# A router's product turned round and split over two halves of TensorE's columns, in a fused encoder layer

## The chip, the cores and the metric

The kernel runs on one core of one Trainium2 chip. All of it is one launch in float32. The metric is the device time of one execution in microseconds; the median over several runs is quoted, and a single execution that the hardware profiler recorded is used for the durations of parts.

## The reference

One layer of a hybrid encoder over 1024 tokens of width 1024: a state-space group and an attention group run side by side, their outputs are mixed by `W_o`, and the normalised sum goes through a mixture of 64 experts of which each token uses 6, plus one shared expert. The part around the change is this:

```python
mix = jnp.concatenate([s, a], axis=-1) @ w_o
x1 = _layer_norm(DEEPNORM_ALPHA * x + mix, ln1_g, ln1_b).astype(x.dtype)
# in _moe, xt = x1 as (1024, 1024):
scores = jax.nn.sigmoid((xt @ w_router).astype(jnp.float32))   # w_router: (1024, 64)
choice = scores + router_bias
# best 4 of 8 groups of experts, then the best 6 experts; weights from scores
...
shared = (jax.nn.silu(xt @ ws_gate) * (xt @ ws_up)) @ ws_down
out = _layer_norm(DEEPNORM_ALPHA * x1 + routed + shared, ln2_g, ln2_b)
```

## The kernel before, in words

The kernel has three stages divided by barriers: projection with attention and state-space scan, then mixing, first norm and routing (`mix_norm_route`), then the experts (`moe_experts`). Each engine has its own program; the order inside an engine is the order written, and engines meet through semaphores (`then_inc`, `wait_ge`). A wait holds back everything behind it on its engine.

In `mix_norm_route` the tokens go by in eight tiles of 128, `t` = 0 to 7. What belongs to a tile:

- `turn_o(t)` on TensorE and `keep_oT(t)` on ScalarE turn the attention output; `mix(t)` makes `p_m`, 16 matmuls of 512 columns: 8 with the turned attention output, then 8 with the state-space output. A float32 matmul is two records in the trace, so a mix is 32 records.
- `norm(t)` on VectorE makes `x1` for the tile. In it the variance goes to ScalarE, whose `deviation(t)` (L1363) takes the square root, and comes back.
- `turn_x(t)` on TensorE (L1274) transposes `x1` in eight blocks into `p_x`; ScalarE copies it to `k.x1T` (L1391).
- `route(t)` on TensorE (L1284) is the router's product: eight matmuls with the tile's `x1T` block as weights (128 by 128) and 64 columns of `w_r` moving, added up in `p_log`, tokens on the partitions. ScalarE's sigmoid (L1397) makes `score`.
- `route(t)` on VectorE picks groups and experts from `score`, makes `member` and the entries' weights; `rank(t)` on TensorE (L1291, L1293) counts tokens per expert; `place(t)` on VectorE (from L1463) turns the rank into a place, and GpSimd scatters the entries (L1225).
- `shared(n, part)` on TensorE (L1094, through `shared_gate_up`) is a quarter of the shared expert's hidden layer in two parts of 16 records each.

TensorE's loop over `t` is: `turn_x(t)`, `turn_o(t + 3)` while there is one, `mix(t + 2)`, `rank(t - 1)`, `route(t)`. In the last two steps there is no mix left, and the order is `turn_x(t)`, `shared(t - 6, 0)`, `rank(t - 1)`, `route(t)`, `shared(t - 6, 1)`. Then come `rank(7)`, one more counting product (L1342) that waits for VectorE's `place(7)` to have read `p_rank`, the other four parts of `shared`, and the transposes of the finished table.

ScalarE's loop is: copy of `x1T` for `t`, `keep_oT(t + 3)`, `deviation(t + 1)` while there is one, the sigmoid of `t`, and in the last two steps the sigmoid of the shared expert's gate. VectorE's is: `norm(t + 1)`, (`hidden(0)` in the last step,) `place(t - 1)`, `route(t)`. SyncE stores `x1` and, when all mixes are through, starts the loads of the first experts' weights into a ring of four places.

Of the kernel before, what the change touches and what calls it, by code (L numbers as in the profile page):

```python
# [6 lines left out]
f32 = mybir.dt.float32  # L7
i32 = mybir.dt.int32
u32 = mybir.dt.uint32
ALU = mybir.AluOpType  # L10
ACT = mybir.ActivationFunctionType
AX = mybir.AxisListType

P = 128
# [5 lines left out]
KD = D // P  # L20
# [11 lines left out]
N_EXPERTS = 64  # L32
# [1082 lines left out]
def mix_norm_route(nc, k):  # L1115

    with ExitStack() as ctx:
        sb, ps, sem = makers(nc, ctx, "mix", k.held)
        w_o = k.mix_w
        w_r = sb("w_r", [P, KD, N_EXPERTS], f32)  # L1120
# [40 lines left out]
        p_x = ps("p_x", [P, KD, P])  # L1161
        p_o = ps("p_o", [P, 512])
        p_log = ps("p_log", [P, 512])
        p_rank, p_log = p_o[:, 0:N_EXPERTS], p_log[:, 0:N_EXPERTS]

        wr_in, ln_in = sem("wr_in"), sem("ln_in")
        blank_done, blank_d, dest_done, scattered = sem("blank_done"), sem("blank_d"), sem("dest_done"), sem("scattered")
# [3 lines left out]
        x_back = [sem(f"x_back{t}") for t in range(T)]  # L1171
        o_turned, oT_done, mixed, mix_read = sem("o_turned"), sem("oT_done"), sem("mixed"), sem("mix_read")
        var_done, std_done, x1_done = sem("var_done"), sem("std_done"), sem("x1_done")
        x_turned, xT_act, logits = sem("x_turned"), sem("xT_act"), sem("logits")
        score_done, member_done, ranked, rank_read, own = sem("score_done"), sem("member_done"), sem("ranked"), sem("rank_read"), sem("own")
        gu_done, sig_done, h_done = sem("gu_done"), sem("sig_done"), sem("h_done")
# [61 lines left out]
        def _(pe):  # L1238
# [9 lines left out]
            def mix(t):  # L1248
                if t == 0:
                    pe.wait_ge(k.mix_w_in, 16)  # L1250
                if t >= 2:
                    pe.wait_ge(mix_read, 2 * t - 2)
                if t == 1:
                    pe.wait_ge(z_sig, 4)
                pe.wait_ge(oT_done, t + 1)
                for half in range(2):
                    cols = slice(half * 512, (half + 1) * 512)
                    for kk in range(4):
                        nc.tensor.matmul(p_m[:, t % 2, cols], oT[:, t % 2, kk, :], w_o[:, 4 + kk, cols], start=(kk == 0), stop=False)
                for half in range(2):  # L1260
                    cols = slice(half * 512, (half + 1) * 512)
                    for kk in range(4):
                        if t == 0 and half == 0:
                            pe.wait_ge(sT_done, kk + 1)
                        last = nc.tensor.matmul(p_m[:, t % 2, cols], k.sT[:, kk, t * P:(t + 1) * P], w_o[:, kk, cols],
                                                start=False, stop=(kk == 3))
                    last.then_inc(mixed, 1)
# [9 lines left out]
            def route(t):  # L1277
                pe.wait_ge(xT_act, t + 1)
                if t == 0:
                    pe.wait_ge(wr_in, 32)  # L1280
                else:
                    pe.wait_ge(score_done, t)
                for kk in range(KD):
                    last = nc.tensor.matmul(p_log, k.x1T[:, kk, t * P:(t + 1) * P], w_r[:, kk, :], start=(kk == 0), stop=(kk == KD - 1))  # L1284
                last.then_inc(logits, 1)

            def rank(t):
                pe.wait_ge(member_done, t + 1)
# [24 lines left out]
            mix(0)  # L1313
            turn_o(2)
            mix(1)
            def shared(n, part):
                if n == 0:
                    pe.wait_ge(k.ws_in, 48)
                if n >= 2:
                    pe.wait_ge(h_done, n - 1)  # L1320
                last = shared_gate_up(nc, k, n, part, p_m[:, n % 2, :])
                if part:
                    last.then_inc(gu_done, 1)

            for t in range(T):
                turn_x(t)
                if t + 3 < T:
                    turn_o(t + 3)
                if t + 2 < T:
                    mix(t + 2)  # L1330
                else:
                    pe.wait_ge(mix_read, 2 * t + 2)
                    shared(t + 2 - T, 0)
                if t:
                    rank(t - 1)
                route(t)
                if t + 2 >= T:
                    shared(t + 2 - T, 1)
            pe.wait_ge(rank_read, T - 1)
# [11 lines left out]
            for g in range(NQ):  # L1351
                last = nc.tensor.transpose(p_x[:, g, 0:COLS], spread[:, g, :, :].rearrange("b q i -> b (q i)"), k.ident[0:COLS, 0:COLS])
            last.then_inc(table_turned, 1)

        @block.scalar
        def _(act):
            def keep_oT(t):
                act.wait_ge(o_turned, t + 1)
                nc.scalar.activation(oT[:, t % 2, :, :].rearrange("p k t -> p (k t)"), p_o[:, :], ACT.Copy).then_inc(oT_done, 1)

            def deviation(t):
                act.wait_ge(var_done, t + 1)
                nc.scalar.activation(std[:, t % 2:t % 2 + 1], mv[:, t % 2, 1:2], ACT.Sqrt).then_inc(std_done, 1)  # L1363

            def gate(n):
                act.wait_ge(gu_done, n + 1)
                if n >= 2:
                    act.wait_ge(h_done, n - 1)
                nc.scalar.activation(sig[:, n % 2, :], p_m[:, n % 2, 0:512], ACT.Sigmoid).then_inc(sig_done, 1)

            def open_gate(m):
                act.wait_ge(z_done, m + 1)
                if m == 0:
                    act.wait_ge(s_done, 4)
                nc.scalar.activation(k.glu_a[m], p_z[m % 2], ACT.Sigmoid, bias=k.glu_b[:, m:m + 1]).then_inc(z_sig, 1)

            gelu_sigmoid(nc, k, 1).then_inc(s_sig, 1)
            gelu_sigmoid(nc, k, 2).then_inc(s_sig, 1)
            nc.scalar.activation(k.glu_a[3], k.glu_s[3], ACT.Square).then_inc(squared, 1)
            keep_oT(0)  # L1380
            act.wait_ge(cubed, 1)
            gelu_sigmoid(nc, k, 3).then_inc(s_sig, 1)
            open_gate(0)
            keep_oT(1)
            for m in range(1, 4):
                open_gate(m)
            keep_oT(2)
            deviation(0)
            for t in range(T):
                act.wait_ge(x_turned, 2 * t + 2)  # L1390
                nc.scalar.activation(k.x1T[:, :, t * P:(t + 1) * P], p_x[:, :, :], ACT.Copy).then_inc(xT_act, 1)  # L1391
                if t + 3 < T:
                    keep_oT(t + 3)
                if t + 1 < T:
                    deviation(t + 1)
                act.wait_ge(logits, t + 1)
                nc.scalar.activation(score[:, t % 2, :], p_log, ACT.Sigmoid).then_inc(score_done, 1)  # L1397
                if t + 2 >= T:
                    gate(t + 2 - T)
            gate(2)  # L1400
            gate(3)

        @block.vector
        def _(dve):
# [90 lines left out]
            for m in range(4):  # L1495
                dve.wait_ge(z_sig, m + 1)
                nc.vector.tensor_tensor(k.sT[:, m, :], k.glu_s[m], k.glu_a[m], ALU.mult).then_inc(sT_done, 1)
            dve.wait_ge(blank_done, 1)
            norm(0)
            for t in range(T):  # L1500
# [506 lines left out]
```

## Time and profile before

| | us |
|---|---|
| median of 3 runs (1530.87 to 1533.76) | 1531.8 |
| the profiled execution | 1530.07 |
| its span | 1528.2 |
| TensorE busy in the span | 1408.0 |
| VectorE busy | 793.8 |
| ScalarE busy | 367.7 |
| GpSimd busy | 612.5 |

The mixing and routing stage takes from about 500 to 732 us of the span, the expert stage all that is behind it. The granted TensorE clock was 0.98 of full speed on average. Times in the rows below are microseconds from the start of the span; a record of TensorE overlaps the next one, so what a group takes is read from its start to the start of the next group, not from its own duration.

### The profile page before, as it was taken

To read this page: it belongs to the slowest core of one execution; us is meant where nothing else is said; L and a number is where in the kernel's file an instruction comes from. 1 tells how busy PE (TensorE), PEld (TensorE's weight loads), DVE (VectorE), ACT (ScalarE), POOL (GpSimd) and SP (SyncE) were. 2 spreads that over 40 slices of the span, in tenths; PEclk is the share of its full clock that TensorE was granted. 3 is DMA by queue.
4 is the path that set the end of the run, shared out by engine and by line. 5 is a ranking of instruction groups with operands and counts; after the bars stand their busy time and mean duration, and the time that the engine had idled before them with its cause. 6 is when DMAs were issued, how large, how long until landed. Compare 5 with 4: busy or idle time off the path is not lost.

```text
span 1528.2 us, 17423 instructions
## 1 busy us (share of the span) xinstructions
PE 1408.0 (92%) x5334; PEld 729.6 (48%) x5334; DVE 793.8 (52%) x1420; ACT 367.7 (24%) x737; POOL 612.5 (40%) x590
## 2 busy tenths in 40 slices
PE   6997999999998999999899999999999999999980
PEld 3544666666666445554344444444444444444430
DVE  3575788888887337884433333333242332323325
ACT  0213555555555312310000101001010100101015
POOL 0008445554430001343345545555554555545520
PEclk9999999999999999999999999999999999999995
DMA  9406101001103630033779999999999999999946
GB/s 233 64 36 75 18 11 19 15 16 19 41 17 123 248 138 29 29 118 135 265 263 370 371 367 370 355 373 361 376 359 371 356 356 374 360 371 362 325 105 234
DMA packets 115342, 321.98 MB, mean 211 GB/s; under 512 B 44390, under 2 KB 65534, under 8 KB 90338
## 3 DMA queue, kind: packets, MB, share of 16 engines
q1 hardware_dynamic: 91890, 261.99, 46.9%
q0 software_dynamic: 23408, 59.45, 16.0%
q8 instruction: 22, 0.36, 0.1%
q14 instruction: 22, 0.18, 0.0%
HBM read 276.45 MB, written 51.72 MB: 215 GB/s over the span
## 4 chain that ended last, share of the span: by engine, by line
DMA 40%; PE 5%; issue 4%; DVE 2%; POOLq 1%; ACT 0%; POOL 0%; ACTq 0%; SPq 0%
DMA sum_d<-moe_y,moe_idx 40%; PE moe_p_gu L1699 2%; PE moe_p_s L1735 2%; PE moe_p_y L1719 1%; DVE all_x_sb L1913 1%; DVE all_x_sb L1908 1%; DMA moe_xg<-x_d,moe_idx 1%; DMA all_x_sb<-sum_d 0%; POOLq L1641 0%; POOL moe_xg L1645 0%; POOL sum_d L1656 0%; POOLq L1682 0%; ACT moe_junk L1815 0%; DVE moe_y L1847 0%; POOLq L1642 0%
## 5 line engine op out<-in xcount | busy, mean ns | idle before, releaser
L1830 DVE STREAM_TRANSPOSE moe_xgT<-moe_xg 128x1024 f32<-128x1024 f32 x65 | 132.0, 2031 | 420.1 <-DMA moe_xg<-x_d,moe_idx 420.1
L1645 POOL DMA_INDIRECT moe_xg<-x_d,moe_idx x260 | 263.7, 1014 | 115.9 <-issue 60.4
L1719 PE MATMUL moe_p_y<-mixers_ring_b,moe_hT 128*128 128x512 f32 x520 | 233.9, 593 | 0.9 <-DVE moe_hT L1841 0.9
L1699 PE MATMUL moe_p_gu<-mixers_ring_b,moe_xgT 128*128 128x512 f32 x512 | 225.0, 593 | 0.0
L1656 POOL DMA_INDIRECT sum_d<-moe_y,moe_idx x65 | 105.7, 1626 | 244.3 <-DMA sum_d<-moe_y,moe_idx 207.5
L1767 ACT ACTIVATE moe_sig<-moe_p_gu 128x256 f32<-128x256 f32 x65 | 24.9, 383 | 585.6 <-PE moe_p_gu L1699 585.6
L1719 PEld LDWEIGHTS moe_p_y<-mixers_ring_b,moe_hT 128*128 128x128 f32 x520 | 98.8, 190 | 124.9 <-issue 123.8
L1699 PEld LDWEIGHTS moe_p_gu<-mixers_ring_b,moe_xgT 128*128 128x128 f32 x512 | 95.2, 191 | 107.1 <-issue 107.1
L1225 POOL DMA_INDIRECT slot_d<-all_entry,all_dest_i x48 | 48.3, 1007 | 224.9 <-DVE all_dest_i L1471 212.7
L709 PE MATMUL att_p_s<-latents_kT,att_qT 128*128 128x512 f32 x256 | 122.8, 603 | 1.1 <-ACT att_v L879 0.7
L1699 PE MATMUL moe_p_gu<-mixers_ring_a,moe_xgT 128*128 128x512 f32 x272 | 119.5, 592 | 0.0
L1699 PE MATMUL moe_p_gu<-mixers_o,moe_xgT 128*128 128x512 f32 x256 | 113.9, 598 | 0.9
L969 DVE TENSOR_REDUCE att_nmax<-att_p_s 128x1 f32<-128x1024 f32 x64 | 78.3, 1224 | 36.0 <-PE att_p_s L709 32.6
L223 POOL TENSOR_TENSOR all_x_sb<-all_x_sb 128x512 f32<-128x512 f32 x32 | 33.8, 1056 | 120.4 <-ACT all_x_sb L209 118.0
L922 ACT ACTIVATE att_prT<-att_p_t 128x512 f32<-128x512 f32 x128 | 69.4, 595 | 40.8 <-PE att_p_t L831 40.8
L1699 PEld LDWEIGHTS moe_p_gu<-mixers_ring_a,moe_xgT 128*128 128x128 f32 x272 | 50.6, 191 | 57.4 <-issue 57.4
L1699 PEld LDWEIGHTS moe_p_gu<-mixers_o,moe_xgT 128*128 128x128 f32 x256 | 47.4, 190 | 57.0 <-issue 57.0
L831 PEld LDWEIGHTS att_p_t<-all_const,att_pr 128*128 128x128 f32 x512 | 59.1, 141 | 29.2 <-issue 29.2
L883 ACT ACTIVATE att_pr<-att_p_s,att_nmax 128x1024 f32<-128x1024 f32 x64 | 70.9, 1108 | 2.3 <-DVE att_nmax L969 2.1
L841 PE MATMUL att_p_o<-att_prT,att_v 128*64 128x128 f32 x1024 | 64.2, 279 | 6.6 <-ACT att_prT L922 6.5
L1773 ACT ACTIVATE moe_y<-moe_p_y,shared_block_w 128x512 f32<-128x512 f32 x65 | 44.7, 688 | 100.7 <-PE moe_p_y L1719 99.4
L831 PE MATMUL att_p_t<-all_const,att_pr 128*128 128x128 f32 x512 | 66.4, 273 | 1.8 <-ACT att_prT L922 1.8
(324 smaller groups left out, 1931.6 us busy)
## 6 DMA issues: line engine op xcount, KB each, us to landing
mixers_ring_b<-in_we_down_dram SPq DMA_DIRECT2D x65, 1024.0 KB, 9.3
mixers_ring_b<-in_we_gate_dram SPq DMA_DIRECT2D x32, 1024.0 KB, 10.2
mixers_ring_b<-in_we_up_dram SPq DMA_DIRECT2D x32, 1024.0 KB, 16.4
mixers_ring_a<-in_we_gate_dram SPq DMA_DIRECT2D x17, 1024.0 KB, 10.0
mixers_ring_a<-in_we_up_dram SPq DMA_DIRECT2D x17, 1024.0 KB, 15.2
mixers_o<-in_we_gate_dram SPq DMA_DIRECT2D x16, 1024.0 KB, 10.1
mixers_o<-in_we_up_dram SPq DMA_DIRECT2D x16, 1024.0 KB, 16.5
moe_xg<-x_d,moe_idx POOLq DMA_INDIRECT x260, 6.9
```

The costliest lines, as they stand in the source:

```text
L709: last = nc.tensor.matmul(p_s[:, t % 2, half * 512:(half + 1) * 512], qT[:, u, t * P:(t + 1) * P], kT[:, u, half * 512:(half + 1) * 512], ...
L831: last = nc.tensor.transpose(p_t[:, j, :], pr[:, t % 2, j * P:(j + 1) * P], k.ident)
L841: last = nc.tensor.matmul(p_o[s * DV:(s + 1) * DV, 0:P], v[:, u, j, :], prT[:, s, j, :], start=(j == 0), stop=(j == T - 1))
L883: nc.scalar.activation(pr[:, t % 2, :], p_s[:, t % 2, :], ACT.Exp, bias=nmax[:, t % 2:t % 2 + 1], accum_out=total[:, t:t + 1]).then_inc(pr ...
L922: nc.scalar.activation(prT[:, t % 2, 4 * half:4 * half + 4, :], p_t[:, 4 * half:4 * half + 4, :], ACT.Copy).then_inc(pT_kept, 1)
L969: nc.vector.tensor_reduce(nmax[:, t % 2:t % 2 + 1], p_s[:, t % 2, :], AX.X, ALU.max, negate=True).then_inc(topped, 1)
L1225: nc.gpsimd.indirect_dma_start(k.slot_d[:, :], bass.IndirectOffsetOnAxis(ap=k.dest[:, n:n + 1], axis=0), k.entry[:, t, q, :], None).then_i ...
L1645: nc.gpsimd.indirect_dma_start(xg[:, u, g, :], None, x1_quarters, bass.IndirectOffsetOnAxis(ap=idx[:, c, g:g + 1], axis=0), bounds_check=N ...
L1656: nc.gpsimd.indirect_dma_start(k.sum_d[:, :], bass.IndirectOffsetOnAxis(ap=idx[:, c, NQ:NQ + 1], axis=0), y[:, u, :], None, compute_op=ALU ...
L1699: last = nc.tensor.matmul(p_gu[:, u, :], xgT[:, u, kk, :], k.moe_gu[v][:, :, kk * F:(kk + 1) * F], start=(kk == 0), stop=(kk == KD - 1))
L1719: last = nc.tensor.matmul(p_y[:, half * 512:(half + 1) * 512], hT[:, u, kk, :], k.moe_dn[v][:, kk * D + half * 512:kk * D + (half + 1) * 512],
L1830: nc.vector.transpose(xgT[:, u].rearrange("p k (g i) -> p g k i", g=NQ), xg[:, u].rearrange("p g (j k) -> p g k j", k=KD)).then_inc(x_turn ...
```

## The change

The router's product is turned: `w_r` (128 by 64) becomes the weights and the tile's `x1T` block (128 columns) moves. The eight blocks of the contraction go in turn to the lower and the upper half of the array's columns, so `p_lt` holds two half sums, each with experts on the partitions. ScalarE copies `p_lt` to `lt`, and a new product `add_halves(t)` with `lt` as weights and two identities of 64 stacked on each other (`both`) gives the sum, turned back, in `p_log`. VectorE builds `both` once. In steps 0 to 5 TensorE's `route(t)` moves to the middle of `mix(t + 2)`, and `add_halves(t)` takes its old place; in steps 6 and 7 `route(t)` stands ahead of `rank(t - 1)` and `add_halves(t)` behind it. ScalarE's copy stands behind `deviation(t + 1)` and ahead of the sigmoid.

```diff
-        p_rank, p_log = p_o[:, 0:N_EXPERTS], p_log[:, 0:N_EXPERTS]
+        both = sb("both", [P, N_EXPERTS], f32)
+        lt = sb("lt", [P, 2, P], f32)
+        p_rank, p_lt, p_log = p_o[:, 0:N_EXPERTS], p_log[:, P:2 * P], p_log[:, 0:N_EXPERTS]
...
                 pe.wait_ge(oT_done, t + 1)
+                routed = t - 2
                 for half in range(2):
                     cols = slice(half * 512, (half + 1) * 512)
                     for kk in range(4):
                         nc.tensor.matmul(p_m[:, t % 2, cols], oT[:, t % 2, kk, :], w_o[:, 4 + kk, cols], start=(kk == 0), stop=False)
+                if routed >= 0:
+                    route(routed)
                 for half in range(2):
...
                 for kk in range(KD):
-                    last = nc.tensor.matmul(p_log, k.x1T[:, kk, t * P:(t + 1) * P], w_r[:, kk, :], start=(kk == 0), stop=(kk == KD - 1))
-                last.then_inc(logits, 1)
+                    s = kk % 2
+                    last = nc.tensor.matmul(p_lt[s * N_EXPERTS:(s + 1) * N_EXPERTS, :], w_r[:, kk, :], k.x1T[:, kk, t * P:(t + 1) * P],
+                                            start=(kk < 2), stop=(kk >= KD - 2))
+                last.then_inc(lt_done, 1)
+
+            def add_halves(t):
+                if t == 0:
+                    pe.wait_ge(both_done, 1)
+                pe.wait_ge(lt_kept, t + 1)
+                nc.tensor.matmul(p_log, lt[:, t % 2, :], both[:, :], start=True, stop=True).then_inc(logits, 1)
...
                     shared(t + 2 - T, 0)
+                    route(t)
                 if t:
                     rank(t - 1)
-                route(t)
+                add_halves(t)
                 if t + 2 >= T:
                     shared(t + 2 - T, 1)
...
                 if t + 1 < T:
                     deviation(t + 1)
+                act.wait_ge(lt_done, t + 1)
+                nc.scalar.activation(lt[:, t % 2, :], p_lt, ACT.Copy).then_inc(lt_kept, 1)
                 act.wait_ge(logits, t + 1)
                 nc.scalar.activation(score[:, t % 2, :], p_log, ACT.Sigmoid).then_inc(score_done, 1)
...
                 nc.vector.tensor_tensor(k.sT[:, m, :], k.glu_s[m], k.glu_a[m], ALU.mult).then_inc(sT_done, 1)
+            nc.vector.tensor_tensor(both[:, :], k.ident[:, 0:N_EXPERTS], k.ident[:, N_EXPERTS:], ALU.add).then_inc(both_done, 1)
             dve.wait_ge(blank_done, 1)
             norm(0)
```

## Rows read from the trace of the kernel before

**Rows 1.** Chain of waits from 500 us on: start, us, what

```profile
731.93 29.54 PE moe_p_s L1735 x64
...
782.23 10.96 DMA sum_d<-moe_y,moe_idx
```

**Rows 2.** One stretch, busy us (records) of PE, PEld, DVE, ACT, POOL; PEclk, DMA, GB/s

```profile
628.00:645.00 17.00, 17.00 (x64) 9.35 (x63) 14.19 (x49) 4.50 (x6) 6.09 (x6) 1.00 0.09 31
```

**Rows 3.** TensorE in order of time, steps 5 to 7: start, us, what, idle before

```profile
660.47 0.39 PE L1293 MATMUL mix_p_o<-mix_seen,all_const 128*128 128x64 f32 x2
660.70 1.95 PE L1284 MATMUL mix_p_log<-mix_w_r,mixers_ring_b 128*128 128x64 f32 x16
662.48 1.09 PE L1274 MATMUL mix_p_x<-all_const,all_x_sb 128*128 128x128 f32 x8
663.41 7.03 PE L1094 MATMUL mix_p_m<-mixers_ring_b,mix_gu 128*128 128x512 f32 x16
670.28 0.33 PE L1291 MATMUL mix_p_o<-mix_member,all_const 128*128 128x64 f32 x2
...
670.67 1.95 PE L1284 MATMUL mix_p_log<-mix_w_r,mixers_ring_b 128*128 128x64 f32 x16
672.46 7.09 PE L1094 MATMUL mix_p_m<-mixers_ring_b,mix_gu 128*128 128x512 f32 x16
...
687.13 0.33 PE L1291 MATMUL mix_p_o<-mix_member,all_const 128*128 128x64 f32 x2
...
698.00 0.44 PE L1342 MATMUL mix_p_o<-mix_seen,all_const 128*128 128x64 f32 x2 [1.21 <-DVE mix_hots L1463]
698.27 27.69 PE L1094 MATMUL mix_p_m<-mixers_ring_b,mix_gu 128*128 128x512 f32 x64
```

**Rows 4.** VectorE in order of time, the ranks of tiles 4 and 6

```profile
660.90 0.55 DVE L1463 TENSOR_TENSOR mix_hots<-mix_hot,mix_p_o 128x384 f32<-128x384 f32 x1 [1.24 <-PE mix_p_o L1293]
...
687.73 0.56 DVE L1463 TENSOR_TENSOR mix_hots<-mix_hot,mix_p_o 128x384 f32<-128x384 f32 x1 [0.27 <-PE mix_p_o L1293]
```

**Rows 5.** TensorE in order of time, attention, around L841

```profile
416.06 1.06 PE L745 MATMUL att_p_p<-mixers_ring_a,att_vsT 128*128 128x128 f32 x8
416.96 1.88 PE L709 MATMUL att_p_s<-latents_kT,att_qT 128*128 128x512 f32 x4
...
419.55 1.06 PE L745 MATMUL att_p_p<-mixers_ring_a,att_vsT 128*128 128x128 f32 x8
420.54 1.97 PE L841 MATMUL att_p_o<-att_prT,att_v 128*64 128x128 f32 x32
422.43 1.99 PE L709 MATMUL att_p_s<-latents_kT,att_qT 128*128 128x512 f32 x4
```

**Rows 6.** ScalarE in order of time; last, all copies of L908 (ns)

```profile
656.98 0.20 ACT L1363 ACTIVATE mix_std<-mix_mv 128x1 f32<-128x1 f32 x1 [7.88 <-DVE mix_rstd L1421]
...
673.81 0.20 ACT L1363 ACTIVATE mix_std<-mix_mv 128x1 f32<-128x1 f32 x1 [7.88 <-DVE mix_rstd L1421]
674.03 1.28 ACT L1397 ACT_TABLE_LOAD   x1
...
L908 ACT ACTIVATE att_oh<-att_p_o x32: 277/277/278, 155.5 to 496.1; 128x128 f32<-128x128 f32 x32
```

**Rows 7.** TensorE after waits; then stretches of 1 us, columns as in rows 2

```profile
139.25 0.63 PE L732 MATMUL att_p_p<-all_const,att_vs 128*128 128x128 f32 x4 [2.71 <-DVE att_vs L621]
...
149.95 2.04 PE L745 MATMUL att_p_p<-mixers_ring_a,att_vsT 128*128 x8 [4.00 <-DMA mixers_ring_a<-u_d]
...
500.17 1.08 PE L1245 MATMUL mix_p_o<-all_const,mixers_o 128*128 128x128 f32 x4 [3.37 <-PEq L1948]
...
155.00:156.00 1.00, 1.00 (x8) 0.59 (x5) 0.23 (x1) 0.51 (x2) 1.00 (x1) 0.94 0.00 0
506.00:507.00 1.00, 1.00 (x3) 0.41 (x2) 0.96 (x4) 0.00 (x0) 0.00 (x0) 0.65 1.03 426
735.00:736.00 1.00, 1.00 (x3) 0.32 (x2) 0.36 (x1) 0.00 (x0) 0.93 (x1) 0.80 1.00 418
```

More of the change, by code:

```diff
@@ L1173, in mix_norm_route @@
         var_done, std_done, x1_done = sem("var_done"), sem("std_done"), sem("x1_done")
+        both_done, lt_done, lt_kept = sem("both_done"), sem("lt_done"), sem("lt_kept")
         x_turned, xT_act, logits = sem("x_turned"), sem("xT_act"), sem("logits")
```

## Prediction

> **What bounds the kernel now.** I read the chain of waits first. From the barrier that closes the mixing and routing stage (called the stage below) it runs without a gap: 29.5 us of TensorE, then expert after expert a scatter whose landing sets the pace [rows 1]. Nothing behind the barrier is touched, and each load of expert weights there waits for a place that an earlier expert frees, so a stage that ends later or earlier moves the end by as much.
>
> Inside the stage I read the busy times by stretch: over a whole token tile TensorE works 17.00 of 17.00 us while VectorE works 14.19 and ScalarE 4.50 [rows 2]. So up to tile 5 only TensorE time counts. In steps 6 and 7 that is no longer true: instead of a mix of 32 wide records, the rank and the router's product have only 16 of them in front (663.41 to 670.28), and 16 behind (672.46) [rows 3]. VectorE has the same work as ever: from the rank of tile 4 (660.90) it runs without a gap, past the variance of tile 7 which ScalarE awaits until 673.81, to the rank of tile 6 at 687.73, for which it waits only 0.27 us [rows 4, 6]. Then TensorE itself waits 1.21 us for VectorE before its last gapless run of 27.69 us [rows 3]. What is late for that run is late at the barrier.
>
> **Part by part: the product itself.** Removed: 16 matmul records per tile, 660.70 to 662.48 = 1.78 us [rows 3], eight times. They stand one behind another, about 0.11 us each.
> Added, first: 16 records with 64-column weights, two for the lower half of the columns, two for the upper, and so on, each moving 128 columns. The trace of before holds this very pattern: the attention's weighted sum (L841) alternates the two halves in pairs of records with the same shapes, and its 32 records last from 420.54 to 422.43 [rows 5]. With (1.97 - 0.28) / 31 = 0.055 us per record (0.28 being about what one record lasts by itself: the 1.06 us of the eight records of L745 less seven steps of 0.11) the halves do run beside each other. 32 records are then 1.75 us, and 0.14 us is left for going back to whole-width matmuls. Going in costs too: L745 lasts 0.99 us ahead of L841 and 0.90 ahead of L709; and the first whole-width group behind it is 0.11 longer (1.99 against 1.88) [rows 5]. So my price c for one turned product is 16 x 0.055 + 0.14 + 0.09 + 0.11 = 1.22 us. Its floor is 0.87 (no cost of change of width); its ceiling is 16 records in a row at 0.11 plus 0.34, or 2.1 us. I take 1.22, since every term has its row.
> The Trainium skill (TensorEngine Tiling, Key Properties) says that a change of tiling mode drains TensorE, and under Theoretical Speedup that two tiles bring up to 2x; by the 2x alone c would be 1.78 / 2 = 0.89 and the sum at the end 3.1 us in place of 5.4. The rows show 0.34 us of cost at the changes of width, so the trace agrees with the drain and the 2x is not reached.
> Added, second: the product with the stacked identities, two records of 64 columns on whole-width weights, as the second matmul of a rank: 660.47 to 660.70 = 0.23 us [rows 3].
> Balance per tile where nothing waits: 1.78 - 1.22 - 0.23 = 0.33 us gained.
>
> **What hides the rest.** The one VectorE addition that builds the identities lies in the long wait for the first mix, over 2 us, and costs nothing. The copy of the half sums on ScalarE is 0.28 us by the same shape in the attention [rows 6]; in tiles 0 to 5 the turned product sits in the middle of a 13.7 us mix, so the copy has some 7 us until it is needed. It stands behind the next tile's deviation on ScalarE, which comes ahead of the rank there (656.98 to 657.18 in step 5, the rank ending at 660.70) [rows 3, 6]. Queues of DMAs: nothing is moved past SP's or POOL's issues.
>
> **The two steps where it isn't hidden.** Clock times are those of before; R is 660.70, where the rank of tile 4 is done. VectorE's run from there to the variance of tile 7 has no gap, so it stays tied to R [rows 4].
> Step 6 after the change: identities' product of tile 5 0.23, eight transposes 0.93 (662.48 to 663.41), first shared half 6.87 (663.41 to 670.28), turned product 1.22, rank 0.39 (670.28 to 670.67) [rows 3]: 660.70 + 9.64 = 670.34. Now comes the new wait. The sum of tile 6 needs ScalarE's copy, and in ScalarE's order that copy stands behind the deviation of tile 7, which waits for VectorE until 673.81 and takes 0.20 [rows 6]. 673.81 + 0.20 + 0.28 + some 0.05 of handing over = 674.34. TensorE stands still for about 3.8 us, since its last matmul drains until about 670.5; queued behind it is the second shared half. The product then takes 0.27 as a lone one (698.00 to 698.27), so that half starts at 674.61, where it started at 672.46: 2.15 us late. Before, the sigmoid stood behind the same deviation, but no TensorE instruction waited for it.
> The table of the sigmoid is loaded behind the deviation (674.03, 1.28 us) [rows 6]. I take it that it will stand behind the copy too, ahead of the sigmoid that it is for; ahead of the copy it would add 1.3 us, which I keep for the range.
>
> **The clock.** After a wait of 2.71 us four matmuls of 128 columns take 0.63 us in all, after one of 3.37 us they take 1.08: the granted clock is then 0.5, 1.2 GHz, the lower of its two levels. From the clock in stretches of 1 us it is back at 1.00 (2.4 GHz) at 506.7 and, after a wait of 4.00 us, at 155.1, that is 6.5 and 5.2 us after the restarts at 500.17 and 149.95; behind the barrier (731.93) it took until 735.4, 3.5 us [rows 1, 7]. A wait of 3.8 us lies between two that did it. Half of 5.1 us, their mean, is lost: 2.5 us (1.75 to 3.25).
> The Trainium skill (TensorE: Matmul & The Clock Gate, "Why this matters for your kernels") advises against idle gaps between bursts of matmuls, since the clock falls in them. The restarts of rows 7 agree; were it not so, the sum would be that of the first rival.
>
> Step 7: the half is over 2.15 + 2.5 = 4.65 us late. The turned product of tile 7 stands ahead of the rank of tile 6, where the old product stood behind it: another 1.22. The rank starts 5.87 us after 687.13 [rows 3]. VectorE, which waited 0.27 us for it, starts as much late [rows 4], and its work on the last tile leads to the one product (698.00) that TensorE waits for; TensorE's own work in between (0.39 + a copy's wait + 0.27 + 6.9 us) is shorter than the 10.87 us from 687.13 to 698.00, so VectorE's lateness is what counts. Against this stands what was gained up to R: 5 x 1.78 = 8.90 removed, 6 x 1.22 + 5 x 0.23 = 8.47 added (six turned products lie before R, five sums), so 0.43.
> Sum: 5.87 - 0.43 = 5.4 us longer. Against the profiled execution, 1530.07 us with a span of 1528.2 and 1.9 around it, that is 1535.5. The median of the runs is 1.7 above that execution, so I state 1531.8 + 5.4 = 1537.2, 0.35% slower. About 0.2%, 3.1 us, is what a measurement can tell from no change.
>
> **Rivals.**
> 1. The wait comes, the clock holds: 5.4 - 2.5 = 2.9 us, 1534.7. For it: one drop came only after 3.37 us, so the bound is near 3.8. Against: three of three such waits. Chance 0.16. It lies on the edge of 0.2%.
> 2. The halves take turns instead of running beside each other, so the change doesn't do what it says: c = 2.1. Before R 6 x 2.1 + 1.15 - 8.90 = 4.9 us lost, then 4.65 + 2.1 = 6.8: 11.6 us, 1543.4. Against it stands L841 with the same shapes. Chance 0.05.
> 3. Not slower: the new wait does not bite. It decides at 670.34: the copy would have to be through by then, 4.0 us ahead of where the deviation puts it, as if ScalarE did not keep its order or the last norm came sooner. TensorE would reach the rank of tile 6 0.66 us before 687.13, VectorE is ready only 0.27 sooner; total 0.3 + 0.4 gained with c = 1.22, 0.3 + 2.5 with c = 0.87: 1531.1 down to 1529.0. Against: the row of the deviation and the gapless VectorE. Chance 0.10, most of it within 0.2%.
> 4. The expert stage takes up or adds some us when it starts at another phase of its transfers: anywhere from 1530 to 1541. Chance 0.07; nothing in the chain speaks for it.
> The forecast has 0.62.
>
> **How the numbers follow.** The sum as a function of c is 7c - 3.1 (2.15 + 2.5 + c late, 8.90 - 6c - 1.15 gained). With c at 0.87 the forecast is 2.4 us less, with the clock at its dearest 0.75 more, with the table ahead 1.3 more. The forecast's own range is 1534.4 to 1539; with the first rival, the size of c and a spread of the runs of 1 to 2 us the range is 1533.3 to 1539.6. Slower by over 0.2%: 0.62, half of rival 1, rival 2, part of 4: 0.76. Same: 0.17. Faster: 0.07.
>
> **What would show it.** Right: the turned product in tiles 0 to 5 lasts about 1.0 us from its start to that of the mix's next matmul and the period of a tile falls by 0.3; an idle TensorE of about 3.8 us ahead of the identities' product of tile 6, released by ScalarE, and half the clock behind it; rank of tile 6 near 692.6; barrier 5 us later. Wrong: 16 records that take 1.7 us (rival 2), full clock in the second shared half of step 6 (rival 1), or that half starting before 672 (rival 3).

## The result and the profile after

The changed kernel takes 1537.1 us (median of 14 runs, 1534.98 to 1542.08) against 1531.8 us for the kernel before in the same rounds (14 runs, 1528.06 to 1533.76). The ratio is 1.0037, 95% interval 1.0027 to 1.0047: 0.37% slower. The profiled execution of the changed kernel took 1537.33 us with a span of 1535.4 us, 7.3 us more than that of before. The difference of the medians is 5.3. In the experiments one execution of e2_fill_wait took 3826 us and is left out of its numbers.

| us | before | after |
|---|---|---|
| the profiled execution | 1530.07 | 1537.33 |
| its span | 1528.2 | 1535.4 |
| TensorE busy | 1408.0 | 1411.1 |
| VectorE busy | 793.8 | 795.0 |
| ScalarE busy | 367.7 | 370.0 |
| from the first tile's transposes to the barrier | 172.0 | 179.0 |
| from the barrier to the end of the span | 796.3 | 796.2 |

The last two lines tell where to look: all of it is lost ahead of the barrier. The chain of waits of after takes the same steps behind it as in [rows 1] (start, us, what):

```profile
739.19 30.40 PE moe_p_s L1753 x64
...
790.35 11.48 DMA sum_d<-moe_y,moe_idx
```

A whole token tile, TensorE in order of time (start, us, what, idle before), around the turned product of tile 3:

```profile
610.24 1.09 PE L1280 MATMUL mix_p_x<-all_const,all_x_sb 128*128 128x128 f32 x8
...
611.60 7.03 PE L1263 MATMUL mix_p_m<-mixers_ring_b,mix_oT 128*128 128x512 f32 x16
618.57 1.09 PE L1291 MATMUL mix_p_log<-mixers_ring_b,mix_w_r 128*64 128x128 f32 x16
619.59 7.13 PE L1271 MATMUL mix_p_m<-mixers_ring_b,mixers_ring_a 128*128 128x512 f32 x16
626.56 0.33 PE L1305 MATMUL mix_p_o<-mix_member,all_const 128*128 128x64 f32 x2
...
626.95 0.39 PE L1299 MATMUL mix_p_log<-mix_both,mix_lt 128*128 128x64 f32 x2
627.18 1.09 PE L1280 MATMUL mix_p_x<-all_const,all_x_sb 128*128 128x128 f32 x8
```

The turned product takes 1.02 us to the next group's start (618.57 to 619.59), and each of the two mix groups around it 6.97 (611.60 to 618.57, 619.59 to 626.56), 0.10 us more than the 6.87 of a group without it [rows 3]. From the transposes of one tile to those of the next are 16.94 us (610.24 to 627.18); before, the same two transposes stand 17.28 us apart (611.08 to 628.36).

Steps 6 and 7 and what follows them, the same view; then, in a second fence, ScalarE and VectorE in order of time:

```profile
660.61 1.09 PE L1280 MATMUL mix_p_x<-all_const,all_x_sb 128*128 128x128 f32 x8
...
669.80 0.39 PE L1307 MATMUL mix_p_o<-mix_seen,all_const 128*128 128x64 f32 x2
673.95 0.69 PE L1299 MATMUL mix_p_log<-mix_both,mix_lt 128*128 128x64 f32 x2 [3.76 <-ACT mix_lt L1412]
674.43 9.62 PE L1094 MATMUL mix_p_m<-mixers_ring_b,mix_gu 128*128 128x512 f32 x16
683.89 1.06 PE L1280 MATMUL mix_p_x<-all_const,all_x_sb 128*128 128x128 f32 x8
...
692.77 0.43 PE L1305 MATMUL mix_p_o<-mix_member,all_const 128*128 128x64 f32 x2
...
701.04 0.41 PE L1305 MATMUL mix_p_o<-mix_member,all_const 128*128 128x64 f32 x2 [0.47 <-issue]
...
703.74 0.69 PE L1357 MATMUL mix_p_o<-mix_seen,all_const 128*128 128x64 f32 x2 [2.07 <-issue]
704.23 28.98 PE L1094 MATMUL mix_p_m<-mixers_ring_b,mix_gu 128*128 128x512 f32 x64
```

```profile
673.53 0.20 ACT L1378 ACTIVATE mix_std<-mix_mv 128x1 f32<-128x1 f32 x1 [9.46 <-DVE mix_rstd L1438]
673.64 0.26 ACT L1412 ACTIVATE mix_lt<-mix_p_log 128x128 f32<-128x128 f32 x1
673.91 1.28 ACT L1414 ACT_TABLE_LOAD   x1
...
693.47 0.56 DVE L1480 TENSOR_TENSOR mix_hots<-mix_hot,mix_p_o 128x384 f32<-128x384 f32 x1 [6.27 <-PE mix_p_o L1307]
```

TensorE stands still for 3.76 us in front of the halves' sum of tile 6 (L1299), until ScalarE's copy, which follows the deviation (673.53) without a gap. VectorE, which waited 0.27 us for the rank of tile 6 in [rows 4], now waits 6.27. Stretches of 1 us, columns as in [rows 2], show the half clock around both waits; by the same view it lasts from 672.7 to 679.5 and from 703.4 to 706.8 us:

```profile
673.00:674.00 1.00, 0.05 (x1) 0.05 (x1) 0.93 (x4) 0.45 (x3) 0.00 (x0) 0.50 0.00 0
...
680.00:681.00 1.00, 1.00 (x4) 0.49 (x3) 0.86 (x5) 0.00 (x0) 0.79 (x1) 1.00 0.95 360
703.00:704.00 1.00, 0.26 (x1) 0.26 (x2) 0.93 (x3) 0.00 (x0) 0.52 (x1) 0.71 0.00 0
...
705.00:706.00 1.00, 1.00 (x2) 0.34 (x1) 0.93 (x4) 0.00 (x0) 0.43 (x1) 0.50 0.00 0
```

### The profile page after: what moved, and what is told of

It is laid out like the page before. It is cut to its first block, busy times and chain, and to the rows that moved or that the text cites. A ratio compares the mean times of both kernels' runs of the same rounds, so it can differ in the third digit from the quotient of the medians.

```text
span 1535.4 us, 17465 instructions
## 1 busy us (share of the span) xinstructions
PE 1411.1 (92%) x5350; PEld 726.1 (47%) x5350; DVE 795.0 (52%) x1421; ACT 370.0 (24%) x745; POOL 613.5 (40%) x590
## 4 chain that ended last, share of the span: by engine, by line
DMA 39%; PE 6%; issue 3%; DVE 2%; POOLq 1%; ACT 0%; POOL 0%; ACTq 0%; SPq 0%
DMA sum_d<-moe_y,moe_idx 39%; PE moe_p_gu L1717 3%; PE moe_p_s L1753 2%; PE moe_p_y L1737 1%; DVE all_x_sb L1931 1%; DVE all_x_sb L1926 1%; DMA moe_xg<-x_d,moe_idx 1%; DMA all_x_sb<-sum_d 0%; POOLq L1659 0%; POOL moe_xg L1663 0%; PE moe_p_h L1725 0%; POOL sum_d L1674 0%; POOLq L1700 0%; ACT moe_junk L1833 0%; DVE moe_y L1865 0%
## 5 line engine op out<-in xcount | busy, mean ns | idle before, releaser
L841 PE MATMUL att_p_o<-att_prT,att_v 128*64 128x128 f32 x1024 | 65.4, 283 | 6.6 <-ACT att_prT L922 6.4
```

Source lines behind the costliest of these rows:

```text
L841: last = nc.tensor.matmul(p_o[s * DV:(s + 1) * DV, 0:P], v[:, u, j, :], prT[:, s, j, :], start=(j == 0), stop=(j == T - 1))
```

## The experiments

All kernels below were timed in rounds with the kernel before on the same chip. "To the barrier" is the time from the first tile's transposes to the barrier in the profiled execution; it leaves out what an execution spends elsewhere. Behind the barrier the profiled executions of the nine kernels below take from 793.4 to 798.0 us, though nothing there was changed, so a single span can't show an effect of 1 or 2 us, and the stretch to the barrier can. It is known from one execution of each kernel. The experiments were timed in four batches, each with its own median of the kernel before (1531.6 to 1532.4 us), so medians of different rows are compared by the ratio.

| run | tiles 0 to 5 | transposes of tile 6 to the barrier | to the barrier | median | ratio (95%) |
|---|---|---|---|---|---|
| before | 102.52 | 69.45 | 171.97 | 1531.8 | |
| after | 100.46 | 78.58 | 179.04 | 1537.1 | 1.0037 (1.0027 to 1.0047) |
| e2_fill_wait | 100.47 | 74.30 | 174.77 | 1536.7 | 1.0027 (1.0015 to 1.0039) |
| e3_one_half | 107.46 | 76.75 | 184.21 | 1544.4 | 1.0086 (1.0071 to 1.0100) |
| e1_copy_first | 100.47 | 74.12 | 174.59 | 1535.0 | 1.0022 (1.0012 to 1.0031) |
| e8_scatters_later | 100.46 | 75.06 | 175.52 | 1535.5 | 1.0024 (1.0015 to 1.0033) |
| e6_sum_later | 100.46 | 70.83 | 171.29 | 1532.7 | 1.0002 (0.9992 to 1.0013) |
| e4_before_tail | 102.52 | 68.01 | 170.53 | 1531.8 | 1.0000 (0.9991 to 1.0009) |
| e10_tail_only | 100.47 | 74.41 | 174.88 | 1533.6 | 1.0009 (0.9999 to 1.0018) |
| e7_sum_later_tail | 100.48 | 68.43 | 168.91 | 1529.1 | 0.9981 (0.9968 to 0.9993) |
| e9_split_part | 100.46 | 67.34 | 167.80 | 1527.6 | 0.9976 (0.9964 to 0.9987) |

**Is it the clock? (e2_fill_wait)** Four matmuls into `p_x`, whose contents nobody reads by then, fill TensorE's wait in step 6; the order is untouched.

```diff
                     rank(t - 1)
+                if t == T - 2:
+                    for i in range(4):
+                        nc.tensor.matmul(p_x[...], k.ws_gu[:, i, 0:P], k.x1T[:, i, 0:512], start=True, stop=True)
                 add_halves(t)
```

> The changed kernel with four float32 matmuls of 512 columns (8 records, 3.4 us) into the unused transposes' banks put into TensorE's wait of step 6; their result is overwritten unread. Theory (the wait costs 2.15 us by itself and 2.5 to 3 us by the half clock): the second shared half takes 6.9 us in place of 9.46, the total is 2.6 us less than the changed kernel, about 2.7 above the kernel before, 1534.5. Rival (the clock falls anyway, or its cost is made up for while VectorE works on): same time as the changed kernel, 1537.

TensorE in order of time:

```profile
669.18 3.65 PE L1353 MATMUL mix_p_x<-mixers_ring_b,mix_gu 128*128 128x512 f32 x8
673.10 0.43 PE L1299 MATMUL mix_p_log<-mix_both,mix_lt 128*128 128x64 f32 x2 [0.27 <-ACT mix_lt L1416]
673.37 7.08 PE L1094 MATMUL mix_p_m<-mixers_ring_b,mix_gu 128*128 128x512 f32 x16
680.29 1.05 PE L1280 MATMUL mix_p_x<-all_const,all_x_sb 128*128 128x128 f32 x8
...
700.13 0.43 PE L1361 MATMUL mix_p_o<-mix_seen,all_const 128*128 128x64 f32 x2 [2.07 <-issue]
700.40 27.68 PE L1094 MATMUL mix_p_m<-mixers_ring_b,mix_gu 128*128 128x512 f32 x64
```

The sum starts no earlier than the copy allows (673.10), and the group behind it takes 6.92 us (673.37 to 680.29) where it took 9.46 (674.43 to 683.89). So the 2.54 us are the clock's. To the barrier it is 2.8 us more than before; 2.7 was expected. The total does not follow: 1534.5 was expected, and the median of 1536.7 is the rival's 1537. The nine runs fall into 1531.1 to 1534.6 (four, the profiled one among them) and 1536.7 to 1538.8 (five). The profiled execution lacks the second stretch at half clock, although TensorE waits 0.46 and 2.07 us ahead of the 64 records as it does in the changed kernel (0.47 and 2.07): they take 27.68 us here and 28.98 there. Whether that stretch makes the upper group isn't shown.

**Do the halves run beside each other? (e3_one_half)** All eight blocks go to the lower half, the sum contracts over 64.

```diff
-                    s = kk % 2
+                    s = 0
...
-                                            start=(kk < 2), stop=(kk >= KD - 2))
+                                            start=(kk == 0), stop=(kk == KD - 1))
...
-                nc.tensor.matmul(p_log, lt[:, t % 2, :], both[:, :], start=True, stop=True).then_inc(logits, 1)
+                nc.tensor.matmul(p_log, lt[0:N_EXPERTS, t % 2, :], both[0:N_EXPERTS, :], start=True, stop=True).then_inc(logits, 1)
...
-                nc.scalar.activation(lt[:, t % 2, :], p_lt, ACT.Copy).then_inc(lt_kept, 1)
+                nc.scalar.activation(lt[0:N_EXPERTS, t % 2, :], p_lt[0:N_EXPERTS, :], ACT.Copy).then_inc(lt_kept, 1)
```

> The changed kernel with all eight blocks of the contraction on the lower half of the columns, and the sum taken over those 64 rows: turned as before, but nothing beside anything. Theory (the halves run beside each other, which is what makes 16 records cost 0.055 us each): the turned product costs 2.1 us a tile instead of 1.22, the period of a tile grows by 0.88, total by 7c - 3.1 = 11.6 us above the kernel before, or 9 if the shorter wait (2.9 us) no longer lowers the clock: 1541 to 1543.5. Rival (it is the 64-column weights that are cheap, not the two halves): time of the changed kernel, 1537.

```profile
657.65 1.96 PE L1291 MATMUL mix_p_log<-mixers_ring_b,mix_w_r 128*64 128x128 f32 x16
659.54 7.13 PE L1271 MATMUL mix_p_m<-mixers_ring_b,mixers_ring_a 128*128 128x512 f32 x16
...
680.44 0.43 PE L1299 MATMUL mix_p_log<-mix_both,mix_lt 64*128 64x64 f32 x2 [2.58 <-ACT mix_lt L1412]
680.80 7.13 PE L1094 MATMUL mix_p_m<-mixers_ring_b,mix_gu 128*128 128x512 f32 x16
687.77 1.05 PE L1280 MATMUL mix_p_x<-all_const,all_x_sb 128*128 128x128 f32 x8
```

The 16 records take 1.89 us where the two halves took 1.02. The same 16 records with the same shapes differ by 0.87 us only in where they go, so the halves run beside each other. The price of one turned product is then 1.89 + 0.20 for its two neighbours = 2.09, the prediction's ceiling of 2.1. The run is still dearer than expected: tiles 0 to 5 take 7.0 us more than in the changed kernel, 1.17 a tile where 0.88 was expected, and the median is 1544.4 us where 1541 to 1543.5 was. The other 0.3 us a tile lie around the sum, which now has only 64 rows: it takes 0.36 us to the next group (667.00 to 667.36) instead of 0.22, it starts 0.10 later behind the rank, and the transposes behind it last 0.06 longer. So this kernel pays for a second change of shape, and its total is not the price of the unsplit product alone.

**Take the copy out from behind the deviation (e1_copy_first).** ScalarE makes the copy first and the next tile's deviation after it.

```diff
-                if t + 1 < T:
-                    deviation(t + 1)
                 act.wait_ge(lt_done, t + 1)
                 nc.scalar.activation(lt[:, t % 2, :], p_lt, ACT.Copy).then_inc(lt_kept, 1)
+                if t + 1 < T:
+                    deviation(t + 1)
```

> The changed kernel with one edit: ScalarE's copy of the half sums stands ahead of the next tile's deviation instead of behind it. Theory (the wait of TensorE for that copy in step 6, and the half clock behind it, are the loss; with them gone VectorE, which had only 0.27 us to spare, sets the last steps): the wait of 3.76 us and the long shared half of 9.46 us go, the rank of tile 6 comes about 0.3 + 0.3 us ahead of the kernel before, total 0.6 us shorter than before, about 1531.2. Rival (the turned product ahead of the rank of tile 6, or the split of the mix, is the loss): the time stays 3 us or more above the kernel before.

GpSimd, ScalarE and TensorE in order of time:

```profile
670.61 0.97 POOL L1228 DMA_INDIRECT slot_d<-all_entry,all_dest_i  x1 [0.30 <-issue]
...
672.64 0.28 ACT L1410 ACTIVATE mix_lt<-mix_p_log 128x128 f32<-128x128 f32 x1 [8.93 <-remote]
...
672.97 0.43 PE L1299 MATMUL mix_p_log<-mix_both,mix_lt 128*128 128x64 f32 x2 [1.84 <-ACT mix_lt L1410]
673.25 8.78 PE L1094 MATMUL mix_p_m<-mixers_ring_b,mix_gu 128*128 128x512 f32 x16
681.86 1.06 PE L1280 MATMUL mix_p_x<-all_const,all_x_sb 128*128 128x128 f32 x8
```

A miss: 1531.2 us was expected and 1535.0 came, the rival's number but not for the rival's reason. The turned product was over by 670.54, ScalarE had nothing in front, and yet the copy began at 672.64, put down to no engine ("remote"). It begins 1.06 us after the end of GpSimd's last scatter, one of tile 4 (670.61 + 0.97 = 671.58). The copies of tiles 2 to 6 all came so, 1.6 to 2.3 us late and 0.96 to 1.10 us behind the last scatter; those of tiles 0, 1 and 7, with no scatter in flight, began at once. And the wait of only 1.84 us that was left still brought half clock: the group behind it took 8.61 us (673.25 to 681.86).

**Is it the scatters? (e8_scatters_later)** As e1_copy_first, and GpSimd's scatters of tiles 0 to 4 wait for the copy of the tile two later.

```diff
+                if t <= 4:
+                    pool.wait_ge(lt_kept, t + 3)
```

> The kernel with the copy ahead of the deviation, and GpSimd's scatters of tiles 0 to 4 held back until ScalarE's copy two tiles later is through, so that no scatter is under way at a copy. In the run without this the copies of tiles 2 to 6 began 1.6 to 2.3 us after the turned product was done and 1.0 us after GpSimd's last scatter; those of tiles 0, 1 and 7, with no scatter about, at once. Theory (a copy waits for the scatters, by whatever way): all copies begin within 0.1 us of the product, TensorE's wait in step 6 falls from 1.84 us to under 0.3, full clock behind it, total 0.6 us below the kernel before, 1531.2. Rival (the delay belongs to the copy's place in ScalarE's queue or to its bank of sums): the delays stay at 1.6 us or more, total 3.3 us above the kernel before.

```profile
670.16 0.28 ACT L1412 ACTIVATE mix_lt<-mix_p_log 128x128 f32<-128x128 f32 x1 [5.92 <-PE mix_p_log L1293]
...
670.53 0.39 PE L1301 MATMUL mix_p_log<-mix_both,mix_lt 128*128 128x64 f32 x2
670.76 7.09 PE L1094 MATMUL mix_p_m<-mixers_ring_b,mix_gu 128*128 128x512 f32 x16
677.68 1.05 PE L1282 MATMUL mix_p_x<-all_const,all_x_sb 128*128 128x128 f32 x8
...
688.53 0.28 ACT L1412 ACTIVATE mix_lt<-mix_p_log 128x128 f32<-128x128 f32 x1 [8.74 <-remote]
...
688.86 0.43 PE L1301 MATMUL mix_p_log<-mix_both,mix_lt 128*128 128x64 f32 x2 [1.65 <-ACT mix_lt L1412]
...
701.06 1.17 PE L1094 MATMUL mix_p_m<-mixers_ring_b,mix_gu 128*128 128x512 f32 x1
```

(ScalarE and TensorE in order of time.) On the delay the theory holds: the copies of tiles 0 to 6 now begin at once (670.16), TensorE has no wait at 670.53, the next group takes 6.92 us (670.76 to 677.68). On the time it doesn't: the scatters held back then run back to back until 686.25, the copy of tile 7 is late instead (688.53), TensorE waits 1.65 us there, and later 1.65 and 2.07 us more, with half clock behind. The median is 1535.5 us where 1531.2 was expected. So the delay was moved from tiles 2 to 6 to tile 7. That the start of this copy hangs on scatters in flight is shown by the two runs; how it does so is not.

**Let the sum come later instead (e6_sum_later).** The copy stays where the change put it; in step 6 TensorE draws the second shared half ahead of the sum.

```diff
+                if t == T - 2:
+                    shared(t + 2 - T, 1)
                 add_halves(t)
-                if t + 2 >= T:
+                if t + 2 > T:
                     shared(t + 2 - T, 1)
```

> The changed kernel with one edit: in step 6 TensorE does the second shared half ahead of the product that adds the halves, so that ScalarE's copy has 6.9 us more; ScalarE's order is the changed kernel's. Theory (the loss is TensorE's wait for the copy and the half clock behind it; without them VectorE, with 0.27 us to spare, sets the last steps): no wait and full clock in step 6, the rank of tile 6 is reached ahead of VectorE, total 0.6 us shorter than the kernel before, about 1531.2. Rival (some 3 us of the loss are elsewhere, in the last ranks or the expert stage, as the run with the copy ahead of the deviation could suggest): 3 us above the kernel before, 1535.

```profile
677.72 0.33 PE L1299 MATMUL mix_p_log<-mix_both,mix_lt 128*128 128x64 f32 x2
...
688.28 0.43 PE L1299 MATMUL mix_p_log<-mix_both,mix_lt 128*128 128x64 f32 x2 [0.81 <-ACT mix_lt L1414]
...
698.29 0.43 PE L1359 MATMUL mix_p_o<-mix_seen,all_const 128*128 128x64 f32 x2 [2.07 <-issue]
698.56 1.94 PE L1094 MATMUL mix_p_m<-mixers_ring_b,mix_gu 128*128 128x512 f32 x4
```

The wait of step 6 and its stretch at half clock are gone (677.72), and the 64 records at the end run at full clock although 2.07 us of waiting stand ahead of them here too. That is 7.75 us to the barrier less than after and 0.68 less than before (0.6 expected). In the total this kernel can't be told from the kernel before (1532.7 against 1532.4 in the same rounds, where 0.6 less was expected). The order of two calls carries the whole net loss: of the 9.13 us that the changed kernel loses from the transposes of tile 6 to the barrier, 1.38 are left, and the 2.06 gained in tiles 0 to 5 cover them.

**The last steps (e4_before_tail, e10_tail_only).** In the kernel before and in the changed one, the first half of a later shared part (8 records) goes ahead of `rank(7)` and the second half behind it, ahead of the last counting product, so that neither waits for VectorE.

```diff
+            pe.wait_ge(h_done, 1)
+            gate_part(2, 0, 4)
             rank(T - 1)
+            gate_part(2, 4, KD)
...
-            for n in range(2, 4):
-                for part in range(2):
-                    shared(n, part)
+            shared(2, 1)
+            for part in range(2):
+                shared(3, part)
```

> The kernel before with TensorE's last steps put in another order: the first part of the shared expert's third quarter is drawn ahead, half of it in front of the rank of tile 7 and half behind, in front of the last counting product. Theory (TensorE's 1.21 us of waiting for VectorE there is on the path, and VectorE and the scatters have room): that wait goes, total 1.2 us less, about 1530.6. Rival (the later table, scatters and VectorE become the bound, or the expert stage takes it up): same or above 1531.8.

> The changed kernel (copy behind the deviation, halves' sum ahead of the second shared half) with one edit: TensorE's last steps in the order of the run that reordered them in the kernel before, so that neither the rank of tile 7 nor the last counting product waits for VectorE. In the changed kernel these two waited 0.47 and 2.07 us, and 64 records behind them took 1.3 us more than in the kernel before, the product ahead of them 0.2 more, at half the clock. Theory (the 1.5 us of the second stretch at half clock hangs on these two waits, and most executions of the changed kernel have it): 2.6 us of waits and 1.5 us of clock go, from the first tile's transposes to the barrier 179.0 - 4.1 = 174.9 us; total 1537.1 - 4.1 = 1533.0. Rival 1 (the second stretch is in few executions, and the changed kernel's median has little of it): the profiled execution as above, but a total of 1534.0 to 1534.7. Rival 2 (the second stretch comes from the first, 20 us earlier, and not from the waits): no waits, but still half clock behind 703 us, 176.4 us to the barrier, 1534.5.

In the kernel before it takes 1.44 us off the way to the barrier (1.2 expected) and nothing that the total can show: 1530.6 was expected, 1531.8 came. In the changed kernel it takes 4.16 us off (174.88; 174.9 expected) and 3.6 us off the median; by the ratios, each against the kernel before in its own rounds, it is 0.28% or 4.3 us. From the rank of tile 6 to the barrier it is 41.95 us against 46.42, 4.47 less: 2.54 of waits, 1.5 of clock, 0.4 more than I can assign; the slow group of step 6 took 0.33 more in this execution:

```profile
674.90 0.69 PE L1299 MATMUL mix_p_log<-mix_both,mix_lt 128*128 128x64 f32 x2 [3.75 <-ACT mix_lt L1421]
675.38 9.95 PE L1094 MATMUL mix_p_m<-mixers_ring_b,mix_gu 128*128 128x512 f32 x16
...
705.12 0.33 PE L1305 MATMUL mix_p_o<-mix_member,all_const 128*128 128x64 f32 x2
...
709.00 0.33 PE L1366 MATMUL mix_p_o<-mix_seen,all_const 128*128 128x64 f32 x2
```

Step 6 still has its wait of 3.75 us and a slow group, but behind it nothing waits, and from 701 to 716 us the clock is 1.00. Rival 2 of that run (the second stretch comes from the first) is out by three more traces: e1_copy_first has the first stretch without the second (27.68 us for the 64 records), and e3_one_half and e8_scatters_later have the second (29.38 and 29.15 us) without the first. How many executions of the changed kernel have the second stretch is not shown: the ratio's interval, 0.9999 to 1.0018, is 3 us wide and holds both the theory (1533.0) and most of rival 1 (1534.0 to 1534.7).

**Both, and the rest of step 7 (e7_sum_later_tail, e9_split_part).** The first is e6_sum_later with the last steps in the new order. The second also draws half of the second shared half of step 7 (4 of 8 matmuls) ahead of the sum of tile 7.

```diff
+                if t == T - 1:
+                    up_part(1, 0, 4)
                 add_halves(t)
                 if t + 2 > T:
-                    shared(t + 2 - T, 1)
+                    up_part(1, 4, KD).then_inc(gu_done, 1)
```

> The same, and TensorE's last steps in the other order that was tried on the kernel before (half of a shared part ahead of the rank of tile 7, half behind it). Theory (VectorE held back what the turned product saves; here TensorE has work for that time): from the rank of tile 4 to the barrier 67.6 us where the kernel before took 71.2, and 0.3 us gained ahead of it, 3.9 us less in total, about 1527.9. Rival (the table and the scatters, 6.3 us ahead of TensorE before, become the bound, or the expert stage takes it up as it seemed to do with the 1.4 us of the run on the kernel before): 1530 to 1531.5.

> The same kernel as the one with the halves' sum later and the last TensorE steps reordered, and besides it, in step 7, half of the second shared part (4 of its 8 matmul instructions, about 1.8 us of TensorE) is drawn ahead of the halves' sum of tile 7. There TensorE waited 0.87 us for ScalarE's copy of that tile's upper half. Theory (the wait is only the copy's late start): no wait above 0.2 us in front of the halves' sum of tile 7; from the first tile's transposes to the barrier 3.9 us less than before, 168.1 us; total 1527.9. Rival 1 (VectorE gets the scores of tile 7 about 1 us later and the ranking of tile 7 ends the stage instead): a wait for VectorE of 1 us or more in front of the last two steps, 168.9 us or more, total 1529.0 or above. Rival 2 (nothing of it is seen in the total, since the part behind the barrier varies by more): 1528.3 to 1530.

TensorE in order of time, e9_split_part (the sum of tile 7, then `rank(7)` and the last counting product):

```profile
691.24 0.33 PE L1299 MATMUL mix_p_log<-mix_both,mix_lt 128*128 128x64 f32 x2
...
698.33 0.33 PE L1305 MATMUL mix_p_o<-mix_member,all_const 128*128 128x64 f32 x2
...
702.21 0.33 PE L1377 MATMUL mix_p_o<-mix_seen,all_const 128*128 128x64 f32 x2
```

In the first, 3.06 us of the expected 3.9 came; what is missing is about the wait of 0.87 us ahead of the sum of tile 7, for the copy of tile 7, which again starts some 1.0 us after the last scatter and 1.1 us after its product. The median is 1529.1 us (1527.9 expected). In the second that wait is gone, and VectorE, which gets the scores of tile 7 later, makes nobody wait: 4.17 us less than before to the barrier (3.9 expected), 1527.6 us (1527.9 expected), 0.24% faster than before with an interval that excludes 1. The gain of the turned product in tiles 0 to 5 is 2.06 us of that; the last steps bring the rest. The new order of the last steps alone brings 1.44 us in the kernel before (e4_before_tail), so 2.73 us to the barrier are left for the new form with its own orders of calls. The kernel before with half a shared part ahead of its step 7 was not tried.

## Why the prediction was right

The prediction was 1537.2 us, the median is 1537.1, and the case is the forecast's, not a rival's. Its steps one by one:

- **The turned product's price c.** 1.22 predicted; measured 1.02 to the next group plus 0.10 in each neighbour = 1.22. Rival 2 would have been 2.1, and e3_one_half shows that price (2.09). The attention's alternating records [rows 5] were the right row. The sum product was 0.22 to 0.23, as predicted.
- **Tiles 0 to 5.** 0.33 us gained per tile predicted, 0.34 measured, six times: 2.06 us between the transposes of tile 0 and those of tile 6.
- **The new wait.** About 3.8 us predicted, 3.76 measured, released by ScalarE's copy behind the deviation, with the table load behind the copy (673.91), as taken.
- **The clock.** 2.5 us predicted, 9.46 - 6.92 = 2.54 measured; e2_fill_wait takes it away by filling the wait alone. The Trainium skill (TensorE: Matmul & The Clock Gate, "Why this matters for your kernels") warns of idle gaps between bursts of matmuls, and behind this wait of 3.76 us the trace agrees.
- **The rank of tile 6.** 5.87 us late against R, less 0.43 gained up to R, is 5.44; measured 692.77 - 687.13 = 5.64 [rows 3], of which 0.19 is an earlier shift (the first transposes began at 560.15 instead of 559.96). So 5.45, against the 5.4 of the sum.
- **What the sum left out.** From the rank of tile 6 to the barrier the prediction took the time as unchanged. It grew by 1.6 us: the counting product 0.2, the 64 records 28.98 instead of 27.69 [rows 3], 0.1 ahead of them. The step that failed is the one that carries VectorE's lateness alone to the barrier, because TensorE's own work in between is shorter. It is shorter; but the same move of the turned product ahead of the rank left TensorE idle 0.47 + 2.07 us at the end instead of 1.21, and the clock fell a second time (703 to 707 us). e10_tail_only removes these waits, and its trace has no such drop. That they bring the drop each time is not so: e1_copy_first and e2_fill_wait have 0.46 + 2.07 us at the same place and no drop.

That the median was met nonetheless is partly luck. For the profiled execution the prediction said 1535.5 us and a barrier 5 us later; it took 1537.33 us, and the barrier came 7.3 us later. The profiled executions differ by 7.3 us, as 5.4 + 1.6 + 0.2 asks; the medians differ by 5.3, and the interval of the ratio, 4.1 to 7.2 us, holds both 5.4 and 5.4 + 1.6, so the median can't tell whether the left-out term is in it. The profiled execution of before lay 1.75 us under its median and that of after 0.2 over: 7.3 - 1.75 - 0.2 = 5.3. e10_tail_only puts the second stretch's share of the median, with the waits around it, at 3.6 us, or 4.3 by the ratios, where the profile has 4.16. In which part the profiled execution of before was 1.75 us faster than its median no run shows.

Rival 1 (the clock holds) and rival 3 (the wait doesn't bite) are excluded by the rows at 674.43 and 673.95. For rival 4 nothing speaks: behind the barrier the two profiled executions differ by 0.1 us; since that part varies by 4.6 us among the kernels, one execution of each does not exclude a small share.

## What to carry to other kernels

Price a saved instruction per tile against the steps where the pipeline runs out of cover: here 0.34 us was gained six times and more than 9 us lost from the last two steps to the barrier, most of it (7.75 us came back in e6_sum_later) because the copy that the new form needs stood behind an instruction that waits for another engine. When an edit moves work ahead of the chain that bounds a step, look for the idle time that it opens behind that chain, and count the clock for it too. Once a profile shows the place, try to reorder calls on the engine that waits: here that gave back 7.75 us of the way to the barrier, while moving the copy on ScalarE (4.45 us) ran into the scatters. A kernel with both the new form and new orders beat the one before by 0.24%.

## What was not expected of the hardware

- ScalarE's copy began about 1.0 us after the end of GpSimd's last indirect scatter, though its own input had been ready for 1.6 to 2.3 us (e1_copy_first, five of eight tiles; holding the scatters back removed it for these in e8_scatters_later). The 1.0 us isn't fixed: the copy of tile 7 in e8_scatters_later, behind twelve scatters in a row, began at 688.53, 2.3 us after the last one's end (686.25); its product had ended at 686.62. Other activations weren't late in a batch of scatters: in e8_scatters_later the shared expert's sigmoid began at 677.88, at once behind its matmuls and 0.2 us after a scatter had begun, and the deviation at 673.83, 0.03 us after its input and 0.1 us after another. Why this copy is stays open.
- The granted clock fell to 0.50 after a wait of 1.84 us (e1_copy_first) and after 0.47 + 2.07 us (after), but stayed at 1.00 over 2.58 us in step 6 of e3_one_half, over 2.07 us in e6_sum_later, and over 0.46 + 2.07 us in e1_copy_first and e2_fill_wait. The length of the waits between 1.8 and 2.6 us does not tell which it will be. The fall can also come when TensorE is at work again: in e1_copy_first it restarted at 672.97, and the clock is 1.00 from 672 to 673, 0.72 in the next microsecond and 0.50 after it. Each drop cost 1.3 to 2.9 us, the last in step 6 of e10_tail_only (9.79 us for a group that takes 6.92 at full clock).
- The part behind the barrier, the same in all kernels, took 793.4 to 798.0 us in the profiled executions.
